# mLSTM heads: a new order of spread, weighing and finishing, and the low parts of the stacked queries and keys on GpSimd

## The reference

```python
    def step(carry, xs):
...
        m_t = jnp.maximum(inter, jnp.max(d, axis=-1))
        s = jnp.einsum('bhtd,bhsd->bhts', qc, kc) * jnp.exp(d - m_t[..., None])
...
        num = jnp.einsum('bhts,bhsv->bhtv', s, vc) + w_inter[..., None] * jnp.einsum('bhtd,bhdv->bhtv', qc, C)
        den = jnp.sum(s, axis=-1) + w_inter * jnp.einsum('bhtd,bhd->bht', qc, n)
        h = num / jnp.maximum(jnp.abs(den), jnp.exp(-m_t))[..., None]
```

## Time and profile before

| what | value |
|---|---|
| time, median of 3 runs | 1890.7 us (1890.65 to 1893.2) |
| span of the profiled execution, first to last instruction | 1892.8 us |
| PE busy, share of the span | 94% |
| DVE, ACT, POOL busy | 73%, 55%, 7% |
| the stage of the heads | from 198.8 us to 281.6 us of the span |
| POOL instructions in all | 139 |

### The profile page before, as it was taken

The page is one execution under the profiler, slowest core; times in us unless marked ns, Lnnn a source line. Parts: engine busy times, 40 slices in busy tenths (PEclk is TensorE's granted clock), DMA queues, the critical chain, the costliest instruction groups (busy, mean ns, idle before and its releaser), DMA issues. The chain is left out here.

```text
span 1892.8 us, 23753 instructions
## 1 busy us (share of the span) xinstructions
PE 1775.1 (94%) x8820; PEld 1468.7 (78%) x8820; DVE 1372.5 (73%) x1457; ACT 1032.5 (55%) x1250; POOL 132.3 (7%) x139
## 2 busy tenths in 40 slices
PE   8999779899999997999988869999999999999997
PEld 2788667787787876887877658888888888888886
DVE  4685578654554565776459559898989898989898
ACT  3643554522222225423344448787878787878775
POOL 2351120000000000000003020000000000000002
PEclk9999999899999998999998969999999999999999
DMA  9353263443433552444310439999999999999996
GB/s 319 132 177 112 76 222 106 159 143 135 139 128 134 166 189 89 135 148 151 134 46 1 167 112 383 347 406 350 407 352 406 347 406 347 408 349 408 355 407 220
DMA packets 148808, 436.23 MB, mean 230 GB/s; under 512 B 8394, under 2 KB 31090, under 8 KB 148605
## 3 DMA queue, kind: packets, MB, share of 16 engines
q1 hardware_dynamic: 146232, 430.92, 62.0%
q0 software_dynamic: 1152, 4.19, 0.6%
q10 hardware_dynamic: 1350, 0.11, 0.1%
HBM read 416.59 MB, written 16.25 MB: 229 GB/s over the span
## 5 line engine op out<-in xcount | busy, mean ns | idle before, releaser
L2925 DVE TENSOR_TENSOR w_low<-e_ring,w_high 128x1536 fp32r<-128x1536 f32 x383 | 611.5, 1621 | 85.3 <-ACT w_high L2829 84.1
L2829 ACT ACTIVATE w_high<-e_ring 128x1536 fp32r<-128x1536 f32 (+1 forms) x381 | 520.1, 1380 | 158.5 <-PE ps L2747 135.8
L2745 PE MATMUL ps<-w_high,list_h 128*128 128x512 f32 (+1 forms) x768 | 290.9, 379 | 4.4 <-DVE list_l L2943 4.2
L2747 PE MATMUL ps<-w_high,list_l 128*128 128x512 f32 (+1 forms) x768 | 287.0, 374 | 0.0
L2746 PE MATMUL ps<-w_low,list_h 128*128 128x512 f32 (+1 forms) x768 | 286.9, 374 | 0.0
L1806 ACT ACTIVATE fw_high<-ring 128x1024 fp32r<-128x1024 f32 x62 | 65.7, 1060 | 262.7 <-PE ps L1735 190.7
L1857 DVE TENSOR_TENSOR fw_low<-ring,fw_high 128x1024 fp32r<-128x1024 f32 x62 | 76.0, 1225 | 150.2 <-ACT fw_high L1806 150.2
L2745 PEld LDWEIGHTS ps<-w_high,list_h 128*128 128x128 f32 x768 | 144.9, 189 | 26.3 <-issue 4.6
L2747 PEld LDWEIGHTS ps<-w_high,list_l 128*128 128x128 f32 x768 | 144.7, 188 | 21.1
L2746 PEld LDWEIGHTS ps<-w_low,list_h 128*128 128x128 f32 x768 | 145.0, 189 | 20.6
L1733 PE MATMUL ps<-u_high,fw_high 128*128 128x512 f32 x352 | 141.2, 401 | 7.6 <-DVE fw_low L1857 7.6
(11 more groups left out here) (450 smaller groups left out, 3326.8 us busy)
## 6 DMA issues: line engine op xcount, KB each, us to landing
e_ring<-in_e_w_gu_dram SPq DMA_DIRECT2D x96, 1536.0 KB, 8.9
e_ring<-in_e_w_down_dram SPq DMA_DIRECT2D x48, 1536.0 KB, 8.7
bg_area<-in_mod_w_dram SPq DMA_DIRECT2D x72, 512.0 KB, 4.1
e_ring<-in_e_w_gu_dram SPq DMA_DIRECT2D x32, 1024.0 KB, 7.7
ring<-in_f_w_gu_dram SPq DMA_DIRECT2D x22, 1024.0 KB, 7.8
ring<-in_h_w_in_dram SPq DMA_DIRECT2D x10, 2048.0 KB, 8.0
e_ring<-in_e_w_down_dram SPq DMA_DIRECT2D x16, 1024.0 KB, 6.6
ring<-in_m_w_in_dram SPq DMA_DIRECT2D x6, 2048.0 KB, 8.7
```

The source lines that it names most:

```text
L2745: nc.tensor.matmul(out, high[:, f, :], w_high[:, c, :], start=(f == 0), stop=False)
L2747: last = nc.tensor.matmul(out, low[:, f, :], w_high[:, c, :], start=False, stop=(f == total - 1))
L2829: nc.scalar.activation(piece(k.w_high, p), raw_piece(k, p), ACT.Copy).then_inc(S.high_done, 1)
L2925: nc.vector.tensor_tensor(piece(k.w_low, p), raw_piece(k, p), piece(k.w_high, p).bitcast(F32), ALU.subtract).then_inc(S.low_done, 1)
```

## The change

PE now spreads the maxima of the next head's forward turn before values(2h), and those of its backward turn after scores(h+1). DVE weighs both turns of a head first and then finishes the backward turn of the head before and the forward turn of this one. The forward result goes to one of two buffers `forward(h)`, and finishing a backward turn multiplies and adds in four instructions straight into `tok`; POOL's addition is gone. The low parts are made on POOL, two subtractions ahead of the masking of turns 0, 1, 3, 5, 7 and 9. The values of the backward turn lie closer to those of the forward one in PSUM and are made in the order 2, 3, 0, 1.

```diff
-    part = k.ex[:, 4 * HALF:6 * HALF].rearrange("p (b t) -> p b t", b=2)
+    forward = lambda h: k.ex[:, (4 + h % 2) * HALF:(5 + h % 2) * HALF].rearrange("p (i c) -> p i c", i=NT)
-    V_STEP, V_FIRST = 171, (5 * HALF, 6 * HALF + 345)
+    V_STEP, V_FIRST = 171, (5 * HALF, 5 * HALF + 4 * 171)
-    HIGH_IN = {0: (1, "q"), 1: (1, "k"), 3: (2, "q"), 4: (2, "k"), 7: (3, "q"), 8: (3, "k")}
-    LOW_IN = {1: (1, "q"), 2: (1, "k"), 4: (2, "q"), 5: (2, "k"), 8: (3, "q"), 9: (3, "k")}
+    HIGH_IN = {0: (1, "k"), 2: (2, "q"), 4: (2, "k"), 6: (3, "q"), 8: (3, "k")}
+    LOW_IN = {0: (1, "q"), 1: (1, "k"), 3: (2, "q"), 5: (2, "k"), 7: (3, "q"), 9: (3, "k")}
...
-                for i in (0, 1, 2, 3) if d == 0 else (1, 2, 3, 0):
+                for i in (0, 1, 2, 3) if d == 0 else (2, 3, 0, 1):
...
-            for n in range(turns):
-                if n % 2 == 0 and n:
-                    scores(n // 2)
-                    spread_m(n)
-                    spread_m(n + 1)
-                if n:
-                    values(n - 1)
-            values(turns - 1)
+            for h in range(HEADS):
+                last_head = h == HEADS - 1
+                if not last_head:
+                    spread_m(2 * h + 2)
+                values(2 * h)
+                if not last_head:
+                    scores(h + 1)
+                    spread_m(2 * h + 3)
+                values(2 * h + 1)
...
+            high(1, "q")
             for n in range(turns):
                 h, d = n // 2, n % 2
-                if n >= 5 and n % 2:
-                    squares_of((n - 5) // 2)
...
                 if n in HIGH_IN:
                     high(*HIGH_IN[n])
+                if n >= 4 and n % 2 == 0:
+                    squares_of((n - 4) // 2)
...
-                if n >= 2:
-                    dve.wait_ge(added, n // 2)
-                nc.vector.tensor_tensor(part[:, d, :].rearrange("p (i c) -> p i c", i=NT), out_values,
-                                        den.unsqueeze(2).to_broadcast([P, NT, DV]), ALU.mult).then_inc(summed, 1)
+                if d == 0:
+                    nc.vector.tensor_tensor(forward(h), out_values, den.unsqueeze(2).to_broadcast([P, NT, DV]),
+                                            ALU.mult).then_inc(summed, 1)
+                    return
+                dve.wait_ge(summed, n)
+                for i in range(NT):
+                    last = nc.vector.scalar_tensor_tensor(out=k.tok[:, i, h * DV:(h + 1) * DV], in0=value_of(d, i)[:, 0:DV],
+                                                          scalar=den[:, i:i + 1], in1=forward(h)[:, i, :], op0=ALU.mult, op1=ALU.add)
+                last.then_inc(summed, 1)
+
+            for h in range(HEADS):
+                weigh(2 * h)
+                weigh(2 * h + 1)
+                if h:
+                    finish(2 * h - 1)
+                finish(2 * h)
...
+                if n in LOW_IN:
+                    low(*LOW_IN[n], n)
                 pool.wait_ge(probs, 4 * n + 4)
```

More of the change, by code:

```diff
@@ L1146, in mlstm_heads @@
     m_cleared = k.sem("a_m_cleared")
-    masked, summed, own, added = k.sem("a_masked"), k.sem("a_summed"), k.sem("a_chain"), k.sem("a_added")
+    masked, summed, own = k.sem("a_masked"), k.sem("a_summed"), k.sem("a_chain")
     turn_done, squares, rooted, m_split = k.sem("a_turn_done"), k.sem("a_squares"), k.sem("a_rooted"), k.sem("a_m_split")
@@ L1270, in squares_of @@
             def squares_of(h):
-                act.wait_ge(added, h + 1)
+                act.wait_ge(summed, 2 * h + 2)
                 if h >= 2:
@@ L1376, in _, with low @@
         def _(pool):
[L1377 to L1382, removed]
             pool.memset(k.m_both[0:32, :, :].bitcast(F32), 0.0).then_inc(m_cleared, 1)
             pool.memset(k.zero_rows, 0.0).then_inc(zeros_made, 1)
+            def low(pair, what, n):
+                pool.wait_ge(zeros_made, 1)
+                if n:
+                    pool.wait_ge(masked, n)
+                done = low_q if what == "q" else low_k
+                for odd in range(2):
+                    rows = own_rows[odd]
+                    if what == "q":
+                        pool.wait_ge(split_q, 2 * (pair - 1) + odd + 1)
+                    else:
+                        pool.wait_ge(split_k, 2 * (pair - 1) + odd + 1)
+                    if what == "q":
+                        pool.tensor_tensor(stacks(pair, "q_low", odd)[rows, :], k.qk[rows, pair, :],
+                                           words(pair, "q_high", odd)[rows, :], ALU.subtract).then_inc(low_q, 1)
+                    else:
+                        pool.tensor_tensor(k.k_low[rows, :], k.qk[rows, 4 + pair, :],
+                                           words(pair, "k", odd)[rows, :], ALU.subtract).then_inc(low_k, 1)
+                    pool.wait_ge(done, 2 * (pair - 1) + odd + 1)
             for n in range(turns):
                 d = n % 2
+                if n in LOW_IN:
+                    low(*LOW_IN[n], n)
                 pool.wait_ge(probs, 4 * n + 4)
@@ L1394, in _ @@
                                    pattern=[[0, NT], [sign, P]], channel_multiplier=-sign).then_inc(masked, 1)
-                if d == 1 and n > 1:
-                    add(n // 2 - 1)
-            add(HEADS - 1)
 def out_pieces(k, name, unit, n_t, presplit):
```

## The result

The changed kernel took 1900.1 us (median of 6 runs, 1893.8 to 1904.3) against 1893.5 us beside it: 1.0036 of the time before, 95% interval 1.0021 to 1.005. In five more rounds on one chip it was 1.0043 (1.0029 to 1.0058). It is slower by 7 to 8 us, and outside the predicted range. The three runs of the kernel before that the prediction started from had a median of 1890.7 us; with the three added here it is 1893.5. Its profiled execution spans 1898.7 us, 5.9 more than before. From the first scores to the next stage's transposes it takes 88.5 us (198.56 to 287.05) where it was 82.8 (198.82 to 281.60), which is 5.7 of the 5.9.

The account below looks back on a forecast made before the run. The prediction took a ring of hand-overs, with no engine full, to bound the heads' stage. Its terms +0.5 - 1.7 + 1.4 + 0.5 = +0.7 us on 1890.7 gave 1891.4 us, likeliest case 1888.7 to 1893.8, range 1888.0 to 1895.0.

Parts of the forecast that it names:

- The ring: One head's scores to the next: scores, spread, backward values, backward weighing, backward finish, block 3 in series, 8.96 us.
- the step in head 3: Turn 6, where ACT's third-pair copies wait for scores(3) and delay the exponentials: +0.4 us, once.
- The product with a pointer: DVE's 128 x 128 products in the backward finish, taken at the upper estimate of 0.34 us each.
- PE's place of waiting: PE waits in the middle of the forward values for line 1354, the last product of the backward finish.
- The length of PE's wait: PE's wait in the middle of each head's forward values, forecast at 2 to 2.5 us.
- Start, +0.5: Up to scores of head 1: query copies precede ACT's table load, scores(1) at 211.0 us; +0.5, upper end +1.3.
- Heads 2 to 7, +1.4: Five rings of 8.96 us plus 0.4 for ACT's copies, 45.2 us against 43.8: +1.4 us.
- Head 7 to the end, +0.5: One ring without new scores, last values, finish, reciprocal and scaling: 16.6 us against 16.11, +0.5.
- the term from head 1 to head 2, -1.7: Scores of head 1 to scores of head 2: 9.19 us instead of 10.91, no longer waiting for low-key copies.
- The port: Rival: POOL's subtractions hold DVE's weighings, up to 0.84 us each, +6.7 us, 1898.1 us in all; chance 0.07.
- The looser ring: Rival: products or block 3 not in series, a ring of 8.2 us, 1886.1 us in all; chance 0.06.
- The clock rival: Rival: PE's granted clock behind the stage loses or saves some 2.5 us, 1888.9 or 1893.9 us; chance 0.12.

Follow-up runs that it names:

- the third profile: Third profile of the unedited changed kernel, taken with its five rounds on one chip; stage 85.6 us, median 1901.9 us, 1.0043 of the kernel before.
- e13: The changed kernel, unedited, timed again in five rounds on one chip: 1901.9 us, 1.0043 of the kernel before.
- e2: Changed kernel with DVE again finishing the backward turn between the next head's two weighings: 1890.5 us, 0.9978 of the kernel before.
- e12: Kernel before with the low parts on POOL and PE's new order, nothing else: 1887.8 us, 0.9973 of the kernel before.
- e14: Changed kernel with forward value blocks 0 to 2 made twice in PE's wait, five rounds on one chip: 1893.9 us, 1.0012 of the kernel before.
- the first pair: The changed kernel's first timing and profile (1900.1 us, 1.0036) against the first with blocks 0 to 2 made twice in PE's wait (1898.1 us, 1.0024).
- e5: Changed kernel with blocks 0 to 2 made twice in PE's wait, plus ten idle matmuls at the stage's start and end: 1897.8 us, 1.003.
- e1: Changed kernel with forward value blocks 0 to 2 made twice in PE's wait: 1898.1 us, 1.0024 of the kernel before.
- e10: Second profile of the changed kernel with blocks 0 to 2 made twice in PE's wait: stage 84.5 us.
- e7: Changed kernel with the backward finish between the weighings and the first pair's copies behind ACT's first exponentials: 1892.8 us, 0.9981 of the kernel before.

## Why the prediction was wrong

Predicted were 1891.4 us, measured 1900.1. Of these 8.7 us, 2.8 are the kernel before, whose median rose from 1890.7 to 1893.5 with three more runs. Against that kernel the change was forecast at +0.7 us and measured at +6.7, and the stage accounts for 5.7 of it in the profile: start +1.7, head 1 to head 2 -0.5, heads 2 to 7 +3.2, the end +1.4, each rounded. The step that failed is the price of PE's stretches: they were costed at full clock.

**Right.** The ring: 8.96 us predicted, 9.01 measured; the step in head 3 9.36 (8.96 + 0.4) against 9.40 in full-clock profiles; heads 2 to 7 45.2 against 45.5 where the clock held. The product with a pointer, the subtraction on POOL, the unstretched weighing and PE's place of waiting came as written. So did ACT's start: the first weighing came 1.2 us later behind the first scores. The length of PE's wait didn't: 1.64 us instead of 2 to 2.5, though the ring's own sum, 8.96 less PE's 7.2, left only 1.8.

**Wrong: the clock, in three terms.** I costed the stage on PE at full clock from scores(1) on, and allowed for the clock only at the start (an upper end 0.8 us higher) and as a rival of 2.5 us behind the stage.

- *Start, +0.5.* The clock rose at 213.2 us instead of at 210.0, in two of three profiles. Scores of head 1 stood 13.33 us behind the first against 11.67 before: +1.7, beyond even my +1.3, since the scores themselves were at half too. In the third profile, where it rose at 210.3, the term was +0.9.
- *Heads 2 to 7, +1.4.* +3.2 in two profiles, +1.7 in the third.
- *Head 7 to the end, +0.5.* +1.4, in all three: 1.55 of it is the last values at half clock (17.77 against 16.22 with the wait filled).

With the wait filled the stage is 84.6, 84.5 and 84.2 us, 1.4 to 1.8 more than before: that is about what the new ring and start cost by themselves, where I had +0.7. The rest of the stage's loss, 1.4 to 3.9 us, the clock's, was not in the sum. I had the earlier trace rows and saw half clock behind waits of PE, and didn't ask what a ring with one wait of 1.6 to 2.3 us would do to it, because the kernel before, with PE busy for 81% of heads 2 to 7 against 82% in the changed kernel, kept full clock there.

**Wrong: the term from head 1 to head 2, -1.7.** It was -0.5, and -1.1 with the clock up. The spread at 212.31 us of the earlier trace rows is merged among score matmuls that go on behind it, so scores(1) lasts longer than the 1.82 I read; from scores(1) to the backward values it took 2.8 us with the clock up (e13), not 2.15.

**Off with no harm: the last stretch.** At full clock it was 16.2 us, less than before. `scale_all` took 2.29 us in the changed kernel and 3.04 before. Before, it ran beside POOL's last addition (see below); I had taken that addition as costless.

**The rivals.** The port didn't hold the weighings. The looser ring didn't occur, but e2 and e12 show what it would be worth. The clock rival had the right mechanism at the wrong place: behind the stage the profiled spans differ by 0.5 us (1611.6 and 1611.2), and in the stage the clock cost up to 3.9 us, not 2.5.

**What stays open.** In the median of 12 runs filling the wait gives 8 us. In the profiles of e13 and e14 it gives 2.6 us of span: 1.4 in the stage and 4.6 behind it, less 3.4 lost ahead of it, where e14 had more half clock in unchanged work and began the stage at 202.0 us instead of 198.7. In the first pair it is 8.4 us: 3.9 in the stage, 4.2 behind it, 0.3 ahead. So half of the gain or more isn't shown by any experiment here to be the ring's. Whether filling brings it about or it goes with where the later work falls in time wasn't found, and the same doubt holds for how much of the 7 to 8 us by which the changed kernel is slower lies in the stage in runs without a profile: e13's profiled execution took 1897.5 us, the median of its runs is 1901.9. The kernel before alone took 1888.8 to 1902.0 us in 35 runs beside e13, with mean granted clocks of 0.968 and 0.959. What the long half clock at the start depends on wasn't settled: PE waits there 3.05 and 0.68 us where it waited 3.29, and it came with idle matmuls too. Nor was it found why the stretch at 240 us comes in some executions alone.

## What to carry to other kernels

Write down the ring of hand-overs before reordering: a finish put behind a weighing that itself waits for PE closed a ring with two PE stretches in it, and moving it one place up was worth 1 us a head. If a reordering gathers PE's idle time into one wait (2.27 us here), price the work behind it at half clock too, and look for full clock in the stretches rather than assume it. A cheap test is to repeat in the wait matmuls that write the same values again: if the stretch with the wait gets shorter, the clock was part of the loss. Compare the stretch and not only the whole time, since here 6 us of the difference lay in work that nobody had changed.

## What the runs showed of the hardware

`scale_all`, a DVE product of two SBUF inputs, takes 3.04 us beside POOL's two-input addition and 2.29 without it. This row of DVE in the changed kernel answers to the last of the earlier trace rows:

```profile
284.46 2.29 DVE L1136 TENSOR_TENSOR tok<-tok,head_sum 128x2048 f32<-128x2048 f32 x1
```

The 0.75 us fit. Ten of the twelve subtractions of POOL ran beside weighings, which read one input from PSUM; these stayed at 0.688 us in the mean. Both agree with the rule of the Trainium skill (SBUF — State Buffer, "SBUF: two separate sides") that the port pair shared by DVE and GpSimd is locked against a DVE operation with two SBUF inputs, and not against one with a single one.

PE was busy for 10.3 us on end at a granted clock of 0.50 (e5): work alone didn't bring the clock back within this stretch, whereas filling went with full clock in the last values where PE still had it (e1, e10, e14). The length of one wait doesn't decide: full clock held behind 2.23 us in the kernel before and 2.03 us in e13, and half clock came behind 1.27 us in e7.
